# A transformer stack on one core: rotated tiles copied whole out of PSUM, their halves swapped by DMA; a later first statistic; merged score groups

## The reference

```python
h = rmsnorm(x, g)                                   # mean of squares over 1024 channels
q, k, v, z = split(h @ w_in)                        # first layer: attention in windows of 128
# mixing part of the last two layers
sb_q, sb_k, sb_v, df_q, df_k, df_v = split(rmsnorm(x, g) @ w_in[l])
sb_out = stick_breaking_attention(sb_q, sb_k, sb_v) # 8 heads of 64
dq, dk = rope(df_q), rope(df_k)                     # xf * cos + concat(-x2, x1) * sin
attn = softmax(dq1 @ dk1.T) - lam * softmax(dq2 @ dk2.T)   # 4 heads, two maps each, causal by chunks
df_out = rmsnorm(attn @ df_v, g_sub) * (1 - lam_init)
x = x + concat(sb_out, df_out) @ w_o[l]
x = x + relu(rmsnorm(x) @ w_ff1)**2 @ w_ff2
```

## Time and profile before

| | us |
|---|---|
| median of 3 runs | 1594.64 |
| lowest, highest | 1590.38, 1595.12 |
| the profiled execution, device time | 1590.36 |
| its span | 1588.6 |
| PE busy in the span | 1545.2 (97%) |
| DVE, ACT, POOL busy | 893.9, 698.0, 157.7 |

### The profile page before, as it was taken

One profiled execution on the slowest core, in us unless ns is written; L12 is line 12 of the kernel. 1 busy time (PEld: TensorE's weight loads), 2 busy tenths in 40 slices (PEclk: granted clock), 3 DMA queues, 4 the chain that ended last, 5 costly groups with the idle time before them and its releaser, 6 DMA issues.

```text
span 1588.6 us, 20837 instructions
## 1 busy us (share of the span) xinstructions
PE 1545.2 (97%) x7841; PEld 1262.3 (79%) x7841; DVE 893.9 (56%) x1494; ACT 698.0 (44%) x1185; POOL 157.7 (10%) x128
## 2 busy tenths in 40 slices
PE   6999999999999999999999999999999999999998
PEld 5776888877778788888888888778788888888886
DVE  5676557566775775534344346566876534344343
ACT  5355533545463774423223244463774423223232
POOL 3000222023000223000000002000223000000001
PEclk9999999999999999999999999999999999999999
DMA  5211232323212112233323233212112233233231
GB/s 167 73 34 54 80 106 80 106 94 106 80 54 80 54 54 86 97 97 106 104 81 106 81 104 106 80 53 80 41 54 93 80 106 103 90 98 106 79 106 53
DMA packets 127286, 135.62 MB, mean 85 GB/s; under 512 B 2458, under 2 KB 120804, under 8 KB 127204
## 3 DMA queue, kind: packets, MB, share of 16 engines
q1 hardware_dynamic: 126100, 133.19, 25.8%
q0 software_dynamic: 288, 1.05, 0.2%
q10 hardware_dynamic: 816, 0.30, 0.1%
HBM read 132.43 MB, written 2.10 MB: 85 GB/s over the span
## 4 chain that ended last, share of the span: by engine, by line
PE 83%; DVE 6%; ACT 5%; issue 3%; POOL 2%; DMA 0%; ACTq 0%; DVEq 0%; POOLq 0%
PE U L1512 23%; PE U L1514 23%; PE U L1513 23%; PE U L1557 2%; PE U L1559 2%; PE U L1558 2%; POOL acc L545 1%; DVE pr L981 1%; PE Z L1702 1%; PE O L1754 1%; PE T L1727 1%; PE Z L1687 1%; PE O L1739 1%; ACT tb L747 1%; PE Z L1613 1%
## 5 line engine op out<-in xcount | busy, mean ns | idle before, releaser
L1512 PE MATMUL U<-XH,WL 128*128 128x512 f32 x976 | 386.1, 396 | 0.9 <-issue 0.9
L1514 PE MATMUL U<-XH,WH 128*128 128x512 f32 x976 | 380.5, 390 | 0.0
L1513 PE MATMUL U<-XL,WH 128*128 128x512 f32 x976 | 380.0, 389 | 0.0
L1512 PE MATMUL U<-MH,WL 128*128 128x512 f32 x848 | 336.6, 397 | 1.9 <-DVE tb L1378 1.7
L930 DVE TENSOR_TENSOR WL<-raw,WH 128x1024 fp32r<-128x1024 f32 x229 | 292.6, 1279 | 79.1 <-ACT WH L574 69.8
L574 ACT ACTIVATE WH<-raw 128x1024 fp32r<-128x1024 f32 x245 | 255.4, 1049 | 173.3 <-PE U L1514 171.3
L1514 PE MATMUL U<-MH,WH 128*128 128x512 f32 x848 | 330.6, 390 | 0.0
L1513 PE MATMUL U<-ML,WH 128*128 128x512 f32 x848 | 330.3, 389 | 0.0
L1512 PEld LDWEIGHTS U<-XH,WL 128*128 128x128 f32 x976 | 183.2, 188 | 43.8 <-issue 7.4
L1514 PEld LDWEIGHTS U<-XH,WH 128*128 128x128 f32 x976 | 183.2, 188 | 38.7
L1513 PEld LDWEIGHTS U<-XL,WH 128*128 128x128 f32 x976 | 183.4, 188 | 36.3 <-issue 0.2
(11 more groups left out here) (218 smaller groups left out, 1669.4 us busy)
## 6 DMA issues: line engine op xcount, KB each, us to landing
raw<-in_w_ff SPq DMA_DIRECT2D x64, 1024.0 KB, 5.2
raw<-in_w_in SPq DMA_DIRECT2D x24, 1024.0 KB, 5.1
raw<-in_attn_w_in SPq DMA_DIRECT2D x9, 1024.0 KB, 5.1
raw<-in_pool_w_in SPq DMA_DIRECT2D x8, 1024.0 KB, 5.3
raw<-in_w_o SPq DMA_DIRECT2D x8, 1024.0 KB, 5.0
raw<-in_attn_w_out SPq DMA_DIRECT2D x4, 1024.0 KB, 4.9
raw<-in_pool_w_out SPq DMA_DIRECT2D x4, 1024.0 KB, 4.9
xin<-in_x SPq DMA_DIRECT2D x2, 1024.0 KB, 6.6
```

The costliest lines, as they stand in the source:

```text
L1512: mm(o, wl, xh, start=first, stop=False, **kw)
L1513: mm(o, wh, xl, start=False, stop=False, **kw)
L1514: return mm(o, wh, xh, start=False, stop=last, **kw)
```

## The change

1. **Rotated tiles.** ACT makes one copy of the whole bank (128 x 512) to `turnable` or to `sq[:, 0]`, in turn, and counts `rope_copied`. DVE's new `free_bank`, first in the next slot, waits for that and counts `result_taken`. SP then starts four DMAs of 32 partitions each, copy to `tb[:, 0]`, halves swapped, in its own queue among the weight loads. DVE's `take` waits for them (`rope_shifted`), and makes its three passes from SBUF; the sum counts `rope_done`, for which scores wait.
2. **Order in a slot.** On ACT `shifted` comes ahead of `conv`. On DVE the bank is freed first; `take` of a rotated tile comes after `conv`, and in a slot with scores after all three rounds of maxima and `conv`.
3. **Positions.** Scores i = 1 and i = 2 both stand at part 2 (from parts 1 and 3); `df_pv` moves from +13 to +14 and `df_f` from +20 to +18 (d = 3: 18 as before).
4. **First statistic.** It moves to `attn[4]`, the first `q` slot, ahead of its first part; `v` results are copied unscaled, and keys and values are scaled behind the statistic.
5. **Opening.** All seven gain DMAs go to ACT's queue, the halves of x are started back to back with a semaphore each, and PE makes 18 products of `mean_w` (memset first on POOL) with itself ahead of its first wait for them.

```diff
-    attn[2]["steps"].append(use(op="stat", columns=True))
+    attn[4]["steps"].append(use(op="stat", columns=True))
...
-            for i, when in enumerate((0, 1, 3)):
+            for i, when in enumerate((0, 2, 2)):
                 at(first + when, op="df_qk", d=d, i=i)
...
-            out_ = at(first + 13, op="df_pv", d=d)
-            at(first + 13, op="df_sq", d=d, of=out_)
-            at(first + (18 if d == 3 else 20), op="df_f", d=d)
+            out_ = at(first + 14, op="df_pv", d=d)
+            at(first + 14, op="df_sq", d=d, of=out_)
+            at(first + 18, op="df_f", d=d)
...
-                if half == 0:
-                    for dst, src in gains[4:]:
-                        sp.dma_start(dst, src).then_inc(gains_landed, 16)
...
+            def turn_halves(n):
+                sp.wait_ge(rope_copied, n)
+                if n > 1:
+                    sp.wait_ge(rope_done, n - 1)
+                for q in range(4):
+                    o = q ^ 1
+                    sp.dma_start(tb[32 * q:32 * q + 32, 0, :], rope_copy(n)[32 * o:32 * o + 32, :]).then_inc(rope_shifted, 16)
...
+                    while ropes and ropes[0][0] <= 2 * p - 6:
+                        turn_halves(ropes.pop(0)[1])
                     load(p, src, 2 * p - 3, p % 2)
...
-                    for q in range(4):
-                        o = q ^ 1
-                        i = a.activation(tb[32 * q:32 * q + 32, 0, :], U[32 * o:32 * o + 32, s["r"] % 2, :], ACT.Copy)
-                    i.then_inc(rope_shifted, 1)
+                    if n > 2:
+                        act.wait_ge(rope_done, n - 2)
+                    a.activation(rope_copy(n), U[:, s["r"] % 2, :], ACT.Copy).then_inc(rope_copied, 1)
...
-            for dst, src in gains[:4]:
+            for dst, src in gains:
...
+            def free_bank(s, l):
+                if s["kind"] in ("dfk", "dfq"):
+                    dve.wait_ge(result_taken, s["r"])
+                    dve.wait_ge(rope_copied, rope_of_result[s["r"]])
+                    dve.sem_inc(result_taken, 1)
+                else:
+                    for i in range(s["n"]):
+                        take(s, i, l)
...
+            pe.wait_ge(mean_ready, 1)
+            for n in range(18):
+                mm(O[:, 0:P], mean_w[:], mean_w[:], start=True, stop=True)
```

More of the change, by code:

```diff
@@ L292, in build, with rope_copy @@
         swa_t_of = {st["pair"]: st for st in all_steps if st["op"] == "swa_t"}
+        rope_of, rope_of_result = {}, {}
+        for l in range(DEPTH):
+            for w in plan["layer", l]:
+                if w["kind"] in ("dfk", "dfq"):
+                    rope_of[l, w["kind"], w["j"]] = rope_of_result[w["r"]] = len(rope_of) + 1
+        def rope_copy(n):
+            return turnable[:] if n % 2 else sq[:, 0, :]
         def raw_view(t):
@@ L784, in layer_slot @@
                 qk, ts = steps_of(s, "df_qk"), steps_of(s, "df_t")
-                if not qk:
-                    conv(s["t"] + 2)
+                if qk:
+                    for st in ts:
+                        df_evict(st)
+                    shifted(before)
+                    df_exp(qk[0])
+                    conv(s["t"] + 2)
+                    df_exp(qk[1])
+                    for st in steps_of(s, "df_sq"):
+                        df_squares(st, l)
+                        df_rsqrt(st, l)
+                    df_exp(qk[2])
+                    return
+                if before:
+                    shifted(before)
+                conv(s["t"] + 2)
                 for st in steps_of(s, "df_f"):
@@ L1158, in layer_slot @@
                     return
-                frees_scores = at and steps_of(plan["layer", l][at - 1], "stat")
-                if low_here and not df_qk:
-                    conv(s["t"] + 2)
-                for st in steps_of(s, "df_f"):
-                    df_low(st, l)
-                if frees_scores:
-                    finish_before()
+                if before:
+                    free_bank(before, l)
                 if df_qk:
                     df_max(df_qk[0], l)
-                if not frees_scores:
-                    finish_before()
+                    if s["n"] == 2:
+                        take(s, 0, l)
+                    df_max(df_qk[1], l)
+                    df_max(df_qk[2], l)
+                    conv(s["t"] + 2)
+                    finish(before, l)
+                    for st in steps_of(s, "df_sq"):
+                        df_mean(st, l)
+                        df_norm(st, l)
+                    return
                 if at in df_mix[l]:
+                    conv(s["t"] + 2)
                     df_combine(df_mix[l][at], l)
-                if low_here and df_qk:
+                    for st in steps_of(s, "df_f"):
+                        df_low(st, l)
+                    finish(before, l)
+                    return
+                if low_here:
                     conv(s["t"] + 2)
+                if s["kind"][-1] == "v":
+                    take(s, 0, l)
+                finish(before, l)
                 if l == 0 and 2 <= at <= 4:
@@ L1399, in take @@
                 taken.add(r + i)
-                ps = result(r + i)
+                if kind not in ("dfk", "dfq"):
+                    ps = result(r + i)
                 rb = rstd[:, 0:S]
                 if kind in ("dfk", "dfq"):
-                    dve.wait_ge(rope_shifted, rope_of[l, kind, j])
+                    n = rope_of_result[r]
+                    dve.wait_ge(rope_shifted, 64 * n)
                     scale = 0.125 if kind == "dfq" else 1.0
-                    v.scalar_tensor_tensor(out=qk[kind][:, j, :], in0=ps, scalar=scale, in1=cs[:, 0, :], op0=ALU.mult, op1=ALU.mult)
                     after(v.scalar_tensor_tensor(out=tb[:, 0, :], in0=tb[:, 0, :], scalar=scale, in1=cs[:, 1, :], op0=ALU.mult, op1=ALU.mult))
-                    v.tensor_tensor(qk[kind][:, j, :], tb[:, 0, :], qk[kind][:, j, :], ALU.add).then_inc(result_taken, 1)
+                    after(v.scalar_tensor_tensor(out=qk[kind][:, j, :], in0=rope_copy(n), scalar=scale, in1=cs[:, 0, :], op0=ALU.mult, op1=ALU.mult))
+                    v.tensor_tensor(qk[kind][:, j, :], tb[:, 0, :], qk[kind][:, j, :], ALU.add).then_inc(rope_done, 1)
                 elif kind == "sbk":
@@ L1446, in _ @@
                     before = plan["layer", l][at - 1] if 1 <= at <= 17 else None
-                    layer_slot(s, l, at, lambda: finish(before, l), at not in POOL_LOW[l] and not s.get("second"))
+                    layer_slot(s, l, at, before, at not in POOL_LOW[l] and not s.get("second"))
                     if at >= 17:
```

70 lines of the change are left out of this document (28 added, 42 removed).

## The result

| | us |
|---|---|
| before, median of 10 runs | 1591.31 (1590.34 to 1595.12) |
| changed, median of 10 runs | 1598.03 (1596.71 to 1599.81) |
| ratio, changed to before | 1.0041 (95%: 1.0033 to 1.0049) |
| profiled span, before and changed | 1588.6 and 1595.2 |

The account below looks back on a forecast made before the run. PE, busy 97% of the span, was taken to bound the kernel. Terms 0 - 3.3 + 1.25 - 2.2 + 1.6 = -2.6 us gave 1587.7 profiled, about 1592 for the median; range 1584 to 1602.

Parts of the forecast that it names:

- opening: Kernel start: earlier high clock for PE's transposes against gains possibly landing later; 0 us, between -0.8 and +5.8.
- first statistic, to the end of slot 5 with the first scores: First layer: PE's 5.11 us wait becomes 3.9, first scores at 54.9 instead of 58.20; -3.3 us, between -6 and +1.
- layer 0, slots 0 to 5: Layer 0's opening: later residual statistic and maxima, against slot 4's wait gone and merged score groups; +1.25 us.
- layer 1, slots 0 to 5: Layer 1's opening: no residual statistic, slot 4's wait gone and score groups merged; -2.2 us.
- slot 7 to 8, both layers: Mixing layers: the second transpose's eviction waits behind the swapped tile's passes, delaying the third transpose; +0.85 us a layer.
- from slot 9 on: Slots 8 to 10: three old waits go, a 3.1 us wait before the third transpose comes; -0.1 us, later heads 0.
- chance a quarter: First statistic: chance that PE, idle 3.9 us, falls to the lower clock, costing 2.6 us more.
- rival 4: First statistic: the stall only moves and the clock falls with it; -3.3 becomes -0.7, 1594.6 us, no change; chance 0.10.
- Rival 2: Slots 7 and 10: DVE's eviction behind the swap decides; slower from L = 4.9, about 1602 us at 5.2; chance 0.20.
- L: Turned tiles: time from ACT's copy to the landing of the swapped halves, taken as 3.6 us, ends 2.6 and 6.5.
- Rival 1: Turned tiles: swapped halves come quickly; at L = 2.6 the sum is -8.6 us, about 1586; chance 0.24.
- Merging: Score groups in each head: a merged pair saves a switch, 0.29 us per head.

Follow-up runs that it names:

- e2: Changed kernel with the first statistic back in the first v slot, v results scaled on the way out, keys right behind it: 1597.81 us.
- e3: Changed kernel with products nobody reads filling PE's longest gaps, the waits themselves kept: 1593.07 us.
- e6: Changed kernel with DVE, in the first layer, copying v results before a later low part and making the statistic before waiting for the q result: 1588.92 us.
- e1: Changed kernel with DVE's eviction of the second transpose ahead of the turned tile's three passes in slots 7 and 10: 1583.66 us.
- e4: Changed kernel with a second landing place for the swapped halves of the tiles of slots 7 and 9: 1589.43 us.
- e8: Changed kernel with the old opening: three gains between the halves of x on SP's queue, no products before PE's first wait: 1598.30 us.
- e7: Changed kernel with every swap made by eight transfers of 16 partitions in place of four of 32: 1627.45 us.
- e9: e5 with the score groups unmerged, at parts 0, 1 and 3 again: 1581.98 us.
- e10: e5 with the old turned tiles: four ACT copies from PSUM, three passes first in DVE's slot, no swaps: 1587.12 us.
- e5: e1 plus the two first-layer DVE moves of e6: 1573.27 us, ratio to before 0.9884.

## Why the prediction was wrong, step by step

The end of each result on PE is the same event in both traces, so what the distance between the two traces changes by gives each term:

| step | forecast | measured |
|---|---|---|
| opening | 0 | -0.10 |
| first statistic, to the end of slot 5 with the first scores | -3.3 | +0.21 |
| layer 0, slots 0 to 5 | +1.25 | +0.87 |
| layer 1, slots 0 to 5 | -2.2 | -1.60 |
| slot 7 to 8, both layers | +1.7 | +1.72 |
| from slot 9 on, layer 0 | -0.1 | +3.53 |
| from slot 9 on, layer 1 | -0.1 | +1.84 |
| sum | -2.6 | +6.5 |

- *Opening, layer openings, slot 8*: right, each within 0.6 us, and by the mechanisms named. Two notes: PE's first transpose came at 8.6 us, later than the 8 that I had called a sign of being wrong, and the faster transposes made up for it; and in layer 1 the scores of slot 5 waited 0.6 us, which I had at nothing.
- *First statistic*: this step failed, by 3.5 us. The gap was 3.90 us, as said, and its releaser the one named. What failed is "chance a quarter" for the clock. It did fall, 0.57 from 36 to 40 us, and the q result of slot 4 was there at 50.3 and not at my 48.3; DVE's chain behind it took 6.3 us where I gave it 6.6, and so released the first scores 1.8 us later than my 54.9, though still 1.5 us ahead of 58.20. PE waited 2.35 us for that chain, and the clock fell again, 0.50 during the scores, which took the rest. e2 shows the worth of the move (nothing), e3 that the clock is the cause of a good part, e6 that the two orders on DVE are the cause of the gaps. One fall of 2.6 us was rival 4, with a chance of 0.10. The fall behind the 3.90 us came in every trace that has this gap and belonged in the sum; the second is a matter of the execution. Where it did not come (e1, e4, e8) this step measures -1.5 to -1.6 us, so that 1.7 to 1.8 us of the 3.5 are missed in any case, and the rest is that fall.
- *From slot 9 on*: the largest failure, 3.6 and 1.9 us. The chain was right link by link, and each link mis-sized to one side: slot 8's tile done at 456.5 and not 454.6; 4.34 us from the swap's start to the first pass and not 3.6, with issues of 0.60 us; so the wait was 4.17 us and not 3.1 (3.67 in layer 1). From slot 9's copy to the first pass on its halves it took 7.3 us, well over the 4.7 that I had called a sign of being wrong. Then the clock, which this term had not priced at all: three waits that sum to 3.2 had been traded for one of 4.17 and 6.8 us at half clock (3.4 in layer 1). e1 and e4 show the chain, e3 the clock.
- *Rival 2* (the eviction behind the swap decides) is what happened in the mixing layers, with its place right and its threshold wrong: I had the kernel slower from L = 4.9, and it lost at 3.9 to 4.3, since the wait is followed by the low clock and the slope above 3.9 is 12 and not 6 (e7). The first statistic's 3.5 us have their part in that. Rival 1 did not come: the landing was quick (2.0 us), but the issues took the time back.
- *Merging*: mis-sized, 0.29 us a head where 0.42 were measured, and its tie to `df_f` not seen (e9).

The range (1584 to 1602) held the time, in part by luck: its middle stood on a median that was 3.3 us too high. The direction was wrong, and the sum missed by 9.1 us (-2.6 against +6.5): 5.6 of them from slot 9 on, 3.5 at the first statistic. In both, terms of both signs were summed as if a wait costs its length.

What stays open: how the 5 us of e3 divide between the three gaps (its own time for fillers overlaps with the waits), what decides whether the clock falls behind a gap of 1.8 to 3 us, which of the two orders on DVE weighs more in the first layer, and what the new positions and the new order on ACT are worth by themselves.

## What to carry to other kernels

- When a hand-written order puts a *wait for a transfer* ahead of instructions that someone else needs, the price is everything behind that wait: ask of each instruction behind it who is blocked, and put the ones that depend on nothing new in front. Moving one kind of instruction ahead of such a wait was worth 14 us here.
- Price a gap of PE by more than its length. In these traces a wait under 1.7 us cost itself alone. One of 3.5 us and more was followed by 3.4 to 10.2 us at half clock, which cost at most half their length. One in between may or may not bring that: put the fall of the clock into the sum, times a chance.
- A good idea can measure as a loss. The turned tiles are worth 14 us (e10), the merging 9 (e9), the statistic 9 to 10 (e5, e6), and yet their sum stood at +6.7 until the orders on DVE were mended. The three numbers add up to more than the 18 us by which e5 is faster, since each was measured with the others in place: the parts lean on one another, and such numbers must not be summed.

## What the runs showed of the hardware

- Transfers of 64 KB between places on chip, four to a swap: 0.60 us an issue on SP, a median of 2.0 to 2.1 us to land (single ones up to 3.6), with weight loads in the same queue. The Trainium skill ("DMA: Bandwidth & Descriptors", section "Anatomy of one DMA") gives a fixed cost of about 2 us to a transfer on another path, one started by GpSimd; the landing here agrees with it. Eight transfers of 32 KB instead of four land as fast each and take 4.9 to 5.8 us to issue: for transfers this small the number of them, not their bytes, is the cost.
- The granted clock in windows right behind the changed kernel's three longest gaps is 0.50 to 0.57, and 1.00 with products that nobody reads in the gap (e3): idle time, not the kind of work, brought it down. The same gap of 2.35 us brought it down in two traces of five.
- One ACT copy of 128 x 512 out of PSUM takes 0.58 to 0.60 us, as long as one of 32 x 512 (2.40 us for four).
